# A transformer forward pass in three-term float32r products: strided order and aligned operands everywhere, and 512 moving columns at once in three of its stages

## The reference, cut to what matters

```
x = x + concat(attention(h), pool(h)) @ w_out      # h = rms_norm(x); "pin", "qkv", "mix"
u = conv3(rms_norm(x) @ w_up)                      # 2 x 5632 columns: "up"
x = x + (silu(gate(u)) * val(u)) @ w_down          # 5632 -> 2048: "down"
x = concat(16 meta tokens, x)                      # 272 tokens from here on
x = x + even_layer(x)                              # "dt","xbc","ssd","glu" in, "outa","outb" out
x = x + odd_layer(x)                               # "na" (q,k,v,z) in, "naout" out
return rms_norm(x)[16:]
```

## Time and profile before

| | us |
|---|---|
| median of three runs | 2375.08 |
| the profiled execution, its own time | 2376.99 |
| its span, first to last instruction | 2375.2 |
| PE busy in the span | 2352.9 (99%) |
| DVE / ACT / POOL busy | 1751.0 (74%) / 1173.6 (49%) / 582.4 (25%) |
| share of PE in the chain that ended last | 93% |

### The profile page before, as it was taken

One profiled execution on the slowest core, in us unless ns is written; L12 is line 12 of the kernel. 1 busy time (PEld: TensorE's weight loads), 2 busy tenths in 40 slices (PEclk: granted clock), 3 DMA queues, 4 the chain that ended last, 5 costly groups with the idle time before them and its releaser, 6 DMA issues.

```text
span 2375.2 us, 55946 instructions
## 1 busy us (share of the span) xinstructions
PE 2352.9 (99%) x20022; PEld 2322.0 (98%) x20022; DVE 1751.0 (74%) x3054; ACT 1173.6 (49%) x1647; POOL 582.4 (25%) x420
## 2 busy tenths in 40 slices
PE   8999999999999999999999999999999999999998
PEld 8999999999999999999999999999999999999997
DVE  6777877777777655589888878888872566666665
ACT  5444455555555444457666643333544444444453
POOL 0230000000000000013423368777777311111100
PEclk9999999999999999999999999999999999999999
DMA  8654666666666666656555545556555555555553
GB/s 281 212 165 143 207 200 200 203 201 201 199 205 197 201 194 195 190 181 198 177 181 169 181 161 177 175 173 192 176 174 175 187 175 161 171 166 177 164 170 133
DMA packets 152419, 438.55 MB, mean 185 GB/s; under 512 B 32324, under 2 KB 47213, under 8 KB 152189
## 3 DMA queue, kind: packets, MB, share of 16 engines
q1 hardware_dynamic: 148844, 424.68, 55.9%
q0 software_dynamic: 3184, 12.14, 1.8%
q10 hardware_dynamic: 288, 0.30, 0.0%
HBM read 434.88 MB, written 11.09 MB: 188 GB/s over the span
## 4 chain that ended last, share of the span: by engine, by line
PE 93%; DVE 4%; ACT 2%; issue 1%; DMA 0%; SPq 0%; DVEq 0%; ACTq 0%
PE bank L1175 29%; PE bank L1173 29%; PE bank L1174 29%; PE bank L1426 1%; DVE wlo L1642 1%; PE bank L1546 1%; PE bank L1536 1%; DVE c L2064 1%; PE bank L1526 1%; PE bank L1397 1%; DMA x<-x_tok 0%; ACT whi L682 0%; PE bank L1553 0%; PE bank L1271 0%; PE bank L1409 0%
## 5 line engine op out<-in xcount | busy, mean ns | idle before, releaser
L1173 PE MATMUL bank<-xhl,whi 128*128 128x256 f32 (+1 forms) x4494 | 1268.7, 282 | 1.2 <-DVE xhl L1713 1.2
L1175 PE MATMUL bank<-xhl,wlo 128*128 128x256 f32 (+1 forms) x4494 | 1261.8, 281 | 0.0
L1174 PE MATMUL bank<-xhl,whi 128*128 128x256 f32 (+1 forms) x4494 | 1257.6, 280 | 0.0
L1173 PEld LDWEIGHTS bank<-xhl,whi 128*128 128x128 f32 x4494 | 843.8, 188 | 4.1 <-DVE xhl L1713 1.5
L1174 PEld LDWEIGHTS bank<-xhl,whi 128*128 128x128 f32 x4494 | 845.8, 188 | 0.7 <-issue 0.2
L1175 PEld LDWEIGHTS bank<-xhl,wlo 128*128 128x128 f32 x4494 | 844.1, 188 | 0.0
L680 ACT CAST whi<-raw 128x1024 fp32r<-128x1024 f32 x420 | 438.7, 1046 | 372.7 <-PE bank L1175 361.9
L1645 DVE TENSOR_TENSOR wlo<-raw,whi 128x1024 fp32r<-128x1024 f32 x364 | 445.4, 1228 | 187.7 <-ACT whi L682 182.8
L682 ACT CAST whi<-raw 128x1024 fp32r<-128x1024 f32 x364 | 381.1, 1052 | 389.3 <-PE bank L1175 368.4
L620 POOL TENSOR_TENSOR wlo<-raw,whi 128x1024 fp32r<-128x1024 f32 x160 | 383.0, 2402 | 122.3 <-ACT whi L680 122.3
L1642 DVE TENSOR_TENSOR wlo<-raw,whi 128x1024 fp32r<-128x1024 f32 x260 | 319.1, 1228 | 108.6 <-ACT whi L680 105.7
(11 more groups left out here) (281 smaller groups left out, 2704.1 us busy)
## 6 DMA issues: line engine op xcount, KB each, us to landing
raw<-w_up SPq DMA_DIRECT2D x176, 512.0 KB, 4.4
raw<-w_na SPq DMA_DIRECT2D x128, 512.0 KB, 3.8
raw<-w_ssm SPq DMA_DIRECT2D x96, 512.0 KB, 3.9
raw<-w_glu SPq DMA_DIRECT2D x96, 512.0 KB, 3.6
raw<-w_down SPq DMA_DIRECT2D x80, 512.0 KB, 4.2
raw<-w_qkv SPq DMA_DIRECT2D x48, 512.0 KB, 4.5
raw<-w_mix SPq DMA_DIRECT2D x32, 512.0 KB, 4.2
raw<-w_outa SPq DMA_DIRECT2D x32, 512.0 KB, 3.8
```

The lines of the kernel that those rows point to most:

```text
L1173: T.matmul(to_, wh, xh_, start=head, stop=False)
L1174: T.matmul(to_, wh, xl_, start=False, stop=False)
L1175: ins = T.matmul(to_, wl, xh_, start=False, stop=last)
```

## The change

It goes through the whole kernel; in its parts:

1. `by_lines` is used for every one of these products, also before "dt". `spread`, `tiles_of` and `wtile` are gone: all weight chunks lie side by side, 1,024 elements at the start of their buffers.
2. The 272-column activations `xh`, `xl` have `XW` = 320 elements (1,280 bytes) a k-tile, and begin 64 bytes into their buffer, which begins at a multiple of 128.
3. The 256-column ones (`t2`, `f2`) hold the high and the low part of a k-tile next to each other, 2 x 1,024 bytes; `ohl` has 1,024 bytes a k-tile. All of these begin at multiples of 128 bytes, as the weights do.
4. "mix", "up" and "down" use `joined` in place of `product`: two matmuls a k-tile. The high weights are multiplied by high and low part at once, 512 columns, into a whole PSUM bank; the low weights by the high part, 256 columns, are added to the bank's first half.
5. The two halves of the bank are then added. In "up" ScalarE copies the second half to `ug`/`uv` (`low_sum`), VectorE adds the first half (and waits for its own end) and multiplies by `rs`. In "mix" and "down" VectorE adds first one half to `x`, then the other.
6. The restarts are gone. `rs` is one buffer, and the taps of the 31-wide convolution are loaded at "glu" into a buffer of their own by a DMA that GpSimd issues; some other small buffers are moved.

```diff
-GROUP = 2 * P + LINE
-WSLOT = 4 * GROUP
+XW = TOK + 3 * LINE
+JOINED = ("mix", "up", "down")
...
+            def joined(phase, i, j, k, m2, kts, start, stop, to=None, done=True):
...
+                for n_, kt in enumerate(kts):
+                    r, o = kt % 8, 2 * kt * SEQ
+                    wh, wl = whi[s][:, r * P:r * P + P], wlo[s][:, r * P:r * P + P]
+                    head, last = start and n_ == 0, stop and n_ == len(kts) - 1
+                    both_, high_ = by_lines(m2[:, o:o + 2 * SEQ]), by_lines(m2[:, o:o + SEQ])
+                    if last:
+                        T.matmul(by_lines(pb_[:, 0:SEQ]), wl, high_, start=False, stop=False)
+                        ins = T.matmul(by_lines(pb_[:, :]), wh, both_, start=False, stop=True)
+                    else:
+                        T.matmul(by_lines(pb_[:, :]), wh, both_, start=head, stop=False)
+                        ins = T.matmul(by_lines(pb_[:, 0:SEQ]), wl, high_, start=False, stop=False)
...
+                def low_sum(k):                                    # ScalarE, "up"
+                    wait_chunk_done(act, "up", i, 2 * k + 1)
+                    A.copy((ug, uv)[k][:, 2:SEQ + 2], pbank("up", k)[:, SEQ:2 * SEQ]).then_inc(sem("low_out"), 1)
...
+            def halves(i, j, k, out):                              # VectorE, "up", for scaled(...)
+                dve.wait_ge(sem("low_out"), i * 2 + (k + 1))
+                ch.link(V.tensor_tensor(out, pbank("up", k)[:, 0:SEQ], out, ADD))
+                freed("up", i, k, V.tensor_tensor(out, out, rs[0][:, META:TOK], MUL))
...
+                    if phase in JOINED:                            # VectorE, landed()
+                        ch.link(V.tensor_tensor(xt, from_[:, 0:SEQ], xt, ADD))
+                        freed(phase, i, k, V.tensor_tensor(xt, from_[:, SEQ:2 * SEQ], xt, ADD))
```

More of the change, by code:

```diff
@@ L130, in program @@
         raw = [at(f"raw{s}", CW) for s in range(RING)]
[L131 to L135, removed]
+        whi = [at(f"whi{s}", CW, F32R) for s in range(RING)]
+        wlo = [at(f"wlo{s}", CW, F32R) for s in range(RING)]
         x = at("x", KT * TOK)
[L137 to L140, removed]
+        xhl = at("xhl", 2 * KT * XW, F32R)
+        xh, xl = xhl[:, LINE:KT * XW], xhl[:, KT * XW + LINE:2 * KT * XW]
+        LINES = 2 * LINE
+        t2 = xhl[:, LINES:LINES + 2 * KT * SEQ]
         Y = arena[0]
-        Y2 = Y + FT * SEQ * 4
-        arena[0] = Y2 + FT * SEQ * 4 + 256
-        vec = at("vec", NVEC)
+        arena[0] = Y + 2 * FT * SEQ * 4 + 256
+        V0 = arena[0]
+        vec = at("vec", NKEPT)
         ident = at("ident", P)
@@ L1177, in product @@
                     ins.then_inc(sem("chunk_done"), 1)
+            def joined(phase, i, j, k, m2, kts, start, stop, to=None, done=True):
+                if start and phase in ("up", "down"):
+                    pe.wait_ge(sem("bank_free"), tile(phase, i, k) + 1)
+                wait_lo(pe, phase, i, j)
+                s, pb_ = j % RING, to if to else pbank(phase, k)
+                for n_, kt in enumerate(kts):
+                    r, o = kt % 8, 2 * kt * SEQ
+                    wh, wl = whi[s][:, r * P:r * P + P], wlo[s][:, r * P:r * P + P]
+                    head, last = start and n_ == 0, stop and n_ == len(kts) - 1
[6 more added lines that the diff above has]
+                        ins = T.matmul(by_lines(pb_[:, 0:SEQ]), wl, high_, start=False, stop=False)
+                if done:
+                    ins.then_inc(sem("chunk_done"), 1)
             def ktiles(j, per=2, total=16, size=8):
@@ L1205, in _ @@
                 if kt < 2:
-                    wh, wl = wtile(whi[0], kt, False), wtile(wlo[0], kt, False)
-                    o = kt * SEQ
-                    T.matmul(bank[0][:, 0:SEQ], wh, th[:, o:o + SEQ], start=kt == 0, stop=False)
-                    T.matmul(bank[0][:, 0:SEQ], wh, tl[:, o:o + SEQ], start=False, stop=False)
-                    T.matmul(bank[0][:, 0:SEQ], wl, th[:, o:o + SEQ], start=False, stop=False)
+                    wh, wl = whi[0][:, kt * P:kt * P + P], wlo[0][:, kt * P:kt * P + P]
+                    to_, hi_, lo_ = (by_lines(t_) for t_ in (bank[0][:, 0:SEQ], *pair(t2, kt)))
+                    T.matmul(to_, wh, hi_, start=kt == 0, stop=False)
+                    T.matmul(to_, wh, lo_, start=False, stop=False)
+                    T.matmul(to_, wl, hi_, start=False, stop=False)
                 else:
@@ L1302, in mixing @@
             def mixing(n, part, kts, out=None, start=False, stop=False, done=True):
-                product("mix", part, n, n % 2, fh, fl, kts, SEQ, 0, SEQ, start, stop, out, done)
+                joined("mix", part, n, n % 2, f2, kts, start, stop, out, done)
             pe.wait_ge(sem("pool_free"), 4)
@@ L1327, in _ @@
                     pe.wait_ge(sem("bank_free"), tile("mix", 2, j // 2) - 1)
[L1328 removed]
+                joined("mix", 2, j, j // 2, f2, ktiles(j), j % 2 == 0, j % 2 == 1)
             with pe.Fori(3, 8) as i:
@@ L1359, in down @@
                     pe.wait_ge(sem("f_ready"), kts[-1] + 1)
-                    product("down", i, j, j // 6, fh, fl, kts, SEQ, 0, SEQ, j % 6 == 0, j % 6 == 5)
-                    if again and j == 6:
-                        restart()
-            for n in range(4):
-                down(2 * n, True)
-                down(2 * n + 1)
+                    joined("down", i, j, j // 6, f2, kts, j % 6 == 0, j % 6 == 5)
+            with pe.Fori(0, 8) as i:
+                down(i)
             for j in range(4):
@@ L1944, in residual @@
                     ch.end()
-                    with dve.Fori(1, 7) as i:
-                        ch.begin(i, 2, 1)
+                    with dve.Fori(1, 8) as i:
+                        ch.begin(i, 4, 1)
                         body(i)
-                    ch.end(6)
-                    body(7)
-                    ch.end()
+                    ch.end(7)
                 else:
```

192 lines of the change are left out of this document (87 added, 105 removed).

## The result

| | before | after |
|---|---|---|
| median (4 runs each) | 2375.77 | 2354.73 us |
| ratio, with its 95% interval | | 0.9911 [0.9897, 0.9924] |
| span of the profiled execution | 2375.2 | 2354.0 us |

The change gains 21 us where 51.5 were forecast. The direction held, and so did the range, which reached from 9 to 89 us of gain; the size did not.

What follows compares the result with a forecast made beforehand. TensorE, busy 99% of the span with 93% of the chain, was taken as the bound. Gains of 20.0 + 27.9 + 2.0 + 1.6 = 51.5 us off 2377.0 gave 2325.5, as median 2324 us; range 2286 to 2366.

Steps and rivals of the forecast that it cites:

- With the 2.9 ns of rows 4 it is 216.2 ... The lower end is 329.5 ... I take 331.: mix, up, down: a joined k-tile takes 331 ns instead of 340, at least 329.5; 20.0 us gained together.
- The upper end ... 336.6.: mix, up, down: the dearest joined k-tile, with 6.3 ns surplus on 512 columns and 114.1 ns for 256.
- if the strided order has a slow one too: Restarts: removing seven gains 1.6 us; a slow rhythm of strided matmuls, no longer interrupted, was counted only in upper ends.
- Down: VectorE is 58% busy: "down": one more VectorE addition a tile is covered; 704 k-tiles x 9 ns gain 6.3 us (2.4 to 7.4).
- in up ... nearly two engines at 100%: "up": VectorE needs 10.44 us a turn, 0.15 below TensorE; a turn of 10.62 us gains 11.4 us (4.8 to 15.0).
- Rival 3: "up": VectorE takes over, waiting for ScalarE's copy; turn 11.64 us, whole kernel 2396 to 2398 us; chance 0.08.
- 272 columns ... I take 120: Matmuls of 272 columns at 1,280 bytes a k-tile: 120 ns each, between 116.2 and some 124; 27.9 us together.
- glu: 11.3, VectorE limits this: 16.76 are work: "glu": 2,304 x 4.9 = 11.3 us gained; VectorE's 16.76 us work a half turn stays below TensorE's 17.28.
- outa, outb: 1,536 x 4.9 = 7.5: "outa" and "outb": matmuls of 272 columns each 4.9 ns shorter, 7.5 us gained (0 to 13.4).
- pin, qkv 0; naout 2.0.: pin, qkv: strided order costs 1.2 us, expected back elsewhere, so 0; "naout": 116.7 to 114.1 ns, 2.0 us gained.
- Rival 1: 272-column stages: padding buys nothing, strided columns pay 6 to 9 ns whatever their place; 2351.5 us; chance 0.24.
- Rival 4: 256-column matmuls: strided order itself costs 6.3 ns, the pair takes 342 ns; whole kernel 2388 us; chance 0.04.

Runs made afterwards that it cites:

- e3: Changed kernel with the last k-tile of a tile in the same order as all others (512 columns, then 256): 2346.19 us, ratio 0.9878.
- e11: e3 with one k-tile swapped, the last of the value tile of turn 22 of "up": up 476.37 us, down 240.92 us.
- e5: e3 with one k-tile swapped, the last of the second tile of "up": 2344.62 us, one execution.
- e10: e3 with VectorE in "glu" no longer waiting for its own end of the running sum and gate product: 2341.70 us, ratio 0.9856.
- e6: e3 with six of the 31 convolution taps in "glu" left out, so it computes something else: 2341.88 us, glu 278.87 us.
- e7: e3 with "outa" multiplying the padded xh and xl instead of yah and yal, so its result differs: 2346.44 us, outa 95.86 us.
- e4: Changed kernel with operands and output of the joined matmuls in mix, up and down read and written in order: 2386.52 us, ratio 1.0046.
- e8: e3 with operand t2 of pin, qkv and "up" beginning 64 bytes later: 2357.33 us, up 475.05 us, down 240.93 us.
- e9: e8 with two 128 x 128 transposes behind the first chunk of each turn of "down": 2353.76 us, down 236.53 us.

## Why the prediction was wrong, step by step

- **"With the 2.9 ns of rows 4 it is 216.2 ... The lower end is 329.5 ... I take 331."** This is the step that failed: the price of the pair, 331 ns where "up" had 339.1 and "down" 336.8. It is 15.8 of the 30.2 us that the gain fell short, 5.5 by its floor and 10.2 by the slow rhythm of the next point. The floor: rows 4 are plain float32 passes; a surplus of 2.9 ns there says nothing of these products. Where nothing is in the way (e3) a float32r matmul takes 16 columns (6.7 ns) over its own, at 272 and at 512 columns, and the pair is 333.3: 2.3 ns more on each of 2,368 k-tiles, 5.5 us. The row for it was at hand: the 113.3 of 256 columns is 16 columns over too. I had put that down to the load.
- **"The upper end ... 336.6."** The mean was 339.1 in "up" and 336.8 in "down", outside. I priced one distance per kind of matmul, while rows 3 and 6 had made me write of a fast and a slow rhythm; the prediction used that only for the restarts ("if the strided order has a slow one too"). It has: 342 against 333.3. The changed kernel's swap in the last k-tile switches it (e3, e11), which holds it in the slow one for half of "up" and 6 of the 16 tiles of "down": 7.0 and 2.4 us by e3. With mix's share (0.8 against e5) and the 5.5 above, that is 15.7 of the 15.8 us that the joined stages fell short.
- **"Down: VectorE is 58% busy"; "in up ... nearly two engines at 100%".** Right in that VectorE does not bound either; too high in the second, where it is 86% busy. Rival 3's wait is there (18.3 us in 39 waits for ScalarE's copy) and delays nobody: in the whole of "up" of e3 TensorE waits once, 0.3 us.
- **"272 columns ... I take 120".** Right in the middle of every stage with a padded operand, but by luck: it was the middle between a floor that is too low and a price of the old layout, with no row for the new one. Worth 4.1 in the scan, 3.3 in "na".
- **"glu: 11.3, VectorE limits this: 16.76 are work".** 7.2. The 0.51 that I took for a wait is VectorE's own loop end, which comes once a turn. After the change the half turn with the loop end takes VectorE 17.40 us without a wait, more than TensorE's 17.28, and the other one 16.88 (17.63 less the wait of 0.75 for the value's tile). So each waits for the other once a turn. e10 and e6 give 3.3 of the missing 4.1 back.
- **"outa, outb: 1,536 x 4.9 = 7.5".** 1.85. The change pads `xh` and `xl` and gives `ohl` 1,024 bytes a k-tile; `yah`, `yal`, `ybh`, `ybl` stay at 1,088 bytes, as the code shows, and I priced them as if they were padded. They take 122 to 124 ns still. And in e7 a padded operand in "outa" alone did not pay.
- **pin, qkv 0; naout 2.0.** -0.84 and 1.35. Strided 256-column matmuls take 114.7 to 115 wherever their start stands as the weights' does, not 114.1. That is also the 1.6 us that q and z cost in "na".
- **The rivals.** Rival 1 (2351.5) came near the time for a wrong reason: padding is worth 12 us; it was the joined stages that gave little. Rival 4's price exists at about 1 ns for three matmuls, and turns round for two (e4).

The Trainium skill ("TensorE: Matmul & The Clock Gate", Back-to-back issue gap) gives 2.5 ns over the columns for a warm matmul, as the gap of a single one, and says that weight loads change it in a stream. The least that any run here shows for these products, over whole tiles, is 6.7.

Open: what in the chip the two rhythms are, and which breaks turn slow into fast. The swap turned it at the end of some tiles and not of others (e5), the slow rhythm also came without a swap ("mix" in e3, "down" in e8), and why the strided order helps a 512-column matmul was not taken apart. Padding "outa" and "outb" for real, and joining qkv or naout, were not tried.

## What to carry to other kernels

Take the floor of a distance between matmuls from the same kind of matmul at another size, and check whether one fixed surplus fits all sizes: here 16 columns are the least for 256, for 272 and for the pair of 512 and 256. Where distances between equal instructions come in two values, look at them tile by tile before pricing a mean; one instruction out of order may decide which value holds for the next 100 us, and keeping the same order in every k-tile was worth 8.5 us here, with less code. When a matmul gets cheaper, the stage's second engine has to be priced with its loop ends and linked waits in, and two waits of a tenth of a microsecond a half turn can be worth as much as six operations.

## What the runs showed of the hardware that I had not expected

- One stream of identical instructions runs at 333.3 or at 342 ns a k-tile, at a clock of 1.00 and without a wait, depending on what came before (e3, e5, e8, e9, e11). In e11 the 342 ns last for 470 us and over a change of stage.
- Two matmuls of 512 and 256 columns in order take 351 ns (e4), three of 256 in order 340 (before), two in strided order 334 to 342 with the same swap (after) and 333.3 without it (e3).
- VectorE's two operations on `ybh` and `ybl` (272 columns, no PSUM tile in them), when they start while GpSimd subtracts (128 x 1,024, 2.4 us), end only 0.16 or 0.30 us behind the end of a subtraction: 0.30 us becomes up to 2.18, 0.44 up to 2.66 (e3, e7). Operations that read or write PSUM aren't held up. Why, no run here shows.
